# The last layer norm of a two-block transformer kernel: means by one-column products, no copies out of PSUM, and two blocks by ScalarE and GpSimd

## The reference

```python
def _layer_norm(x, g, b):
    xf = x.astype(jnp.float32)
    mu = jnp.mean(xf, axis=-1, keepdims=True)
    var = jnp.mean(jnp.square(xf - mu), axis=-1, keepdims=True)
    return ((xf - mu) * lax.rsqrt(var + LN_EPS) * g + b).astype(x.dtype)
...
        h = x * (1.0 + scale2) + shift2
        y = _conv_ffn(h, w_up[l], conv_w[l], conv_b[l], w_down[l])
        x = _layer_norm(DEEPNORM_ALPHA * x + gate2 * y, ln2_g[l], ln2_b[l])
```

## Time and profile before

| | before |
|---|---|
| median of 3 runs | 1812.11 us (1811.92 to 1812.45) |
| the profiled execution: its time | 1814.47 us |
| the profiled execution: its span | 1812.70 us |
| PE busy, share of the span | 1765.8 us, 97% |
| DVE busy | 972.2 us, 54% |
| ACT busy | 674.5 us, 37% |
| POOL busy | 825.2 us, 46% |
| granted TensorE clock, mean | 0.989 of 2.4 GHz |

### The profile page before, as it was taken

How to read it: one execution, slowest core, us unless ns; L and a number is a source line. 1 busy time by engine, 2 the same in 40 slices (tenths; PEclk the granted TensorE clock), 3 DMA queues, 4 the chain that set the end, 5 groups by cost and what they waited for, 6 DMA issues and landing times. The chain is left out here.

```text
span 1812.7 us, 26173 instructions
## 1 busy us (share of the span) xinstructions
PE 1765.8 (97%) x8981; PEld 1496.2 (83%) x8981; DVE 972.2 (54%) x1608; ACT 674.5 (37%) x1390; POOL 825.2 (46%) x664
## 2 busy tenths in 40 slices
PE   7999999999999999999999999899999899999996
PEld 5888888888777888888888888699988878888886
DVE  4257535668965477152125367466567673552545
ACT  4322222243476433232233233655532552332332
POOL 3553454567970455444545455100034465455450
PEclk9999999999999999999999999999999999999998
DMA  6454452533311345433333333100012134323321
GB/s 203 126 164 151 140 152 81 174 99 111 94 43 40 121 148 188 136 91 107 100 89 107 103 95 93 47 2 1 1 58 83 47 99 134 101 85 105 95 79 47
DMA packets 279700, 178.49 MB, mean 98 GB/s; under 512 B 6264, under 2 KB 258356, under 8 KB 279476
## 3 DMA queue, kind: packets, MB, share of 16 engines
q1 hardware_dynamic: 265348, 149.35, 28.3%
q10 hardware_dynamic: 14256, 27.87, 4.4%
HBM read 175.11 MB, written 2.10 MB: 98 GB/s over the span
## 5 line engine op out<-in xcount | busy, mean ns | idle before, releaser
L630 POOL TENSOR_TENSOR wL<-raw,wH 128x512 fp32r<-128x512 f32 (+2 forms) x560 | 747.6, 1358 | 916.7 <-ACT wH L1358 915.4
L731 PE MATMUL ps<-actH,wH 128*128 128x512 f32 (+1 forms) x1312 | 511.8, 390 | 8.1 <-DVE actL L2254 4.4
L731 PE MATMUL ps<-actH,wL 128*128 128x512 f32 (+1 forms) x1312 | 506.0, 386 | 0.0
L731 PE MATMUL ps<-actL,wH 128*128 128x512 f32 (+1 forms) x1312 | 506.0, 386 | 0.0
L1358 ACT ACTIVATE wH<-raw 128x512 fp32r<-128x512 f32 (+2 forms) x560 | 312.7, 608 | 339.6 <-PE ps L731 337.7
L731 PEld LDWEIGHTS ps<-actH,wH 128*128 128x128 f32 x1312 | 248.3, 189 | 58.8 <-issue 4.5
L731 PEld LDWEIGHTS ps<-actH,wL 128*128 128x128 f32 x1312 | 248.3, 189 | 49.6
L731 PEld LDWEIGHTS ps<-actL,wH 128*128 128x128 f32 x1312 | 248.2, 189 | 49.3 <-issue 0.7
L731 PE MATMUL ps<-hidH,wH 128*128 128x512 f32 (+1 forms) x720 | 267.6, 372 | 0.0
L731 PE MATMUL ps<-hidH,wL 128*128 128x512 f32 (+1 forms) x720 | 266.6, 370 | 0.0
L731 PE MATMUL ps<-hidL,wH 128*128 128x512 f32 (+1 forms) x720 | 266.5, 370 | 0.0
(11 more groups left out here) (320 smaller groups left out, 2037.6 us busy)
## 6 DMA issues: line engine op xcount, KB each, us to landing
mod_raw<-in_w_mod ACTq DMA_DIRECT2D x24, 1024.0 KB, 5.8
raw<-in_w_in SPq DMA_DIRECT2D x48, 512.0 KB, 3.7
raw<-in_ffn_w_gate SPq DMA_DIRECT2D x44, 512.0 KB, 3.9
raw<-in_ffn_w_up SPq DMA_DIRECT2D x44, 512.0 KB, 3.8
raw<-in_w_up SPq DMA_DIRECT2D x44, 512.0 KB, 3.8
raw<-in_ffn_w_down SPq DMA_DIRECT2D x32, 512.0 KB, 3.8
raw<-in_w_out SPq DMA_DIRECT2D x16, 512.0 KB, 3.7
raw<-in_w_down SPq DMA_DIRECT2D x16, 512.0 KB, 3.6
```

Source lines behind the costliest of these rows:

```text
L630: nc.gpsimd.tensor_tensor(wL[:, b:b + w // 2], raw[:, b:b + w // 2], wH[:, b:b + w // 2].bitcast(F32), ALU.subtract).then_inc(lo_ready, 1)
L731: return nc.tensor.matmul(out, a, b, start=first, stop=last)
```

## The change

It does these things:

- The means of the tokens come from TensorE. `mean_columns(pair, b, ks)` multiplies a 128x128 piece of x by one column of `ones` (which holds 1/1024), for two token blocks and the feature tiles `ks`, and puts each result in a column of its own in bank b. VectorE adds the eight columns of a token block with one `tensor_reduce`.
- The blocks of half 1 of the features are no longer copied to SBUF. ACT squares them, and `gained_block` reads them, in PSUM.
- TensorE's transposes move: those of blocks 4 and 5 into the middle of slab 0 of half 1, behind 16 one-column products; two of the four pieces of blocks 6 and 7 to before the last slab, behind 12 products. After the last slab there are four transposes and four products.
- For q = 2 and 3 and half 0 of the features, `gained_block` leaves VectorE: ACT subtracts the mean (`Identity` with a bias, after its squares) and GpSimd multiplies with the gain. `last_block` waits for it.
- `c_bias` is made before the drain of the last slab of half 0; the blocks of q = 1 are finished before the second pair begins.

```diff
+        pool.wait_ge(gb_in, 32)
+        for q in range(2, ST):
+            pool.wait_ge(fin_shift, q - 1)
+            G.tensor_tensor(out_block(q), out_block(q), ln2_gB[:, 0:512], ALU.mult).then_inc(fin_gained, 1)
...
-        def natural(n, tiles, ready):
+        def natural(n, ks=range(4)):
 
             half, q = n // ST, n % ST
-            for k in range(4):
-                pe.wait_ge(*ready(k))
+            for k in ks:
                 mm = nc.tensor.transpose(bank(4 + q, P, k * P), x[:, (4 * half + k) * S + q * P:][:, 0:P], ident)
-            mm.then_inc(fin_T, 1)
+            if 3 in ks:
+                mm.then_inc(fin_T, 1)
+
+        def mean_columns(pair, b, ks):
+
+            for q in (2 * pair, 2 * pair + 1):
+                for k in ks:
+                    mm = product(ps[:, b, (q % 2) * KT + k:][:, 0:1], x[:, k * S + q * P:][:, 0:P], ones[:, 0:1], True, True)
+            if KT - 1 in ks:
+                mm.then_inc(fin_cols, 1)
...
-            def hook(half, j):
-                if half == 0 and j in (1, 2):
+            def hook(half, j, k):
+                if half == 0 and j in (1, 2) and k == K - 1:
+                    pe.wait_ge(drained_v, d0 + 4)
                     for q in (2 * j - 2, 2 * j - 1):
-                        natural(q, range(4), lambda k: (drained_v, d0 + k + 1))
-                if half == 1 and j == 1:
+                        natural(q)
+                if (half, j, k) == (1, 0, 3):
+                    pe.wait_ge(fin_sum, ST)
+                    pe.wait_ge(half_drained, 2 * 4)
+                    mean_columns(0, 6, range(KT))
                     for q in range(2):
-                        pe.wait_ge(fin_sum, q + 1)
-                        natural(ST + q, range(4), lambda k: (half_drained, 4 + k + 1))
+                        natural(ST + q)
+                if (half, j, k) == (1, 2, K - 1):
+                    pe.wait_ge(fin_centre, 1)
+                    pe.wait_ge(drained_v, d0 + 6)
+                    mean_columns(1, 0, range(6))
+                    for q in range(2, ST):
+                        natural(ST + q, (0, 1))
 
             token_halves("f3_down2", ready, K, 4, lambda j, k: None, hook)
-            for q in range(2, ST):
-                pe.wait_ge(fin_sum, q + 1)
-                natural(ST + q, range(4), lambda k: (drained_v, d0 + 4 + k + 1))
+            for k in (2, 3):
+                pe.wait_ge(drained_v, d0 + 4 + k + 1)
+                for q in range(2, ST):
+                    natural(ST + q, (k,))
+                mean_columns(1, 0, (4 + k,))
...
             if n >= ST:
-                act.wait_ge(fin_copy, q + 1)
+                act.wait_ge(fin_T, n + 1)
...
-            nc.scalar.activation(tile(sq2, n % 2), out_block(n), ACT.Square, scale=D ** -0.5, bias=ssq[:, 8 + q:9 + q],
+            nc.scalar.activation(tile(sq2, n % 2), bank(4 + q) if n >= ST else out_block(n), ACT.Square, scale=D ** -0.5, bias=ssq[:, 8 + q:9 + q],
                                  accum_out=ssq[:, 32 + n:33 + n]).then_inc(fin_sq, 1)
+        act.wait_ge(fin_centre, 3)
+        for q in range(2, ST):
+            nc.scalar.activation(out_block(q), out_block(q), ACT.Identity, bias=ssq[:, 20 + q:21 + q]).then_inc(fin_shift, 1)
...
-        def final_mean(q0):
-
-            for q in (q0, q0 + 1):
-                dve.wait_ge(fin_T, ST + q + 1)
-                V.tensor_tensor_reduce(out=out_block(ST + q), in0=bank(4 + q),
-                                       in1=zero[:, 0:1].broadcast_to([P, S]), scale=1.0, scalar=0.0,
-                                       op0=ALU.add, op1=ALU.add, accum_out=rest[:, q:q + 1]).then_inc(fin_copy, 1)
-            dve.wait_ge(fin_copy, q0 + 2)
-            two = slice(q0, q0 + 2)
-            link(V.scalar_tensor_tensor(md[:, two], rest[:, two], 1.0 / D, c_half[:, two], ALU.mult, ALU.add))
-            link(V.tensor_tensor(mu_neg[:, two], c_neg[:, two], md[:, two], ALU.subtract))
+        def final_mean(pair, b):
+
+            two = slice(2 * pair, 2 * pair + 2)
+            dve.wait_ge(fin_cols, pair + 1)
+            V.tensor_reduce(mean[:, two], bank(b, 2 * KT).rearrange("p (q k) -> p q k", q=2), AX_X, ALU.add).then_inc(fin_centre, 1)
+            dve.wait_ge(fin_centre, pair + 1)
+            link(V.tensor_tensor(md[:, two], mean[:, two], c_neg[:, two], ALU.add))
...
+            if half == 0 and q >= 2:
+                dve.wait_ge(fin_gained, q - 1)
             V.scalar_tensor_tensor(o, o, rn[:, q:q + 1], ln2_bB[:, half * 512:half * 512 + 512],
                                    ALU.mult, ALU.add).then_inc(fin_v, 1)
...
-        for j in range(2):
-            half_tile("f3_down2", 1, j, 40, 4)
+        half_tile("f3_down2", 0, 3, 40, 4)
+        half_tile("f3_down2", 1, 0, 40, 4)
         dve.wait_ge(gb_in, 32)
-        final_mean(0)
-        for half in range(2):
-            gained_block(0, half)
+        final_mean(0, 6)
+        gained_block(0, 0)
+        gained_block(1, 0)
+        gained_block(0, 1)
+        half_tile("f3_down2", 1, 1, 40, 4)
+        gained_block(1, 1)
         final_rn(0)
         half_tile("f3_down2", 1, 2, 40, 4)
-        for half in range(2):
-            last_block(0, half)
+        last_block(0, 0)
+        last_block(0, 1)
         half_tile("f3_down2", 1, 3, 40, 4)
-        final_mean(2)
-        for half, q in ((0, 1), (1, 1), (0, 2), (0, 3), (1, 2), (1, 3)):
-            gained_block(q, half)
-        final_rn(2)
-        for q in range(1, ST):
+        last_block(1, 0)
+        last_block(1, 1)
+        final_mean(1, 0)
+        V.tensor_scalar(ssq[:, 22:24], mean[:, 2:4], -1.0, None, ALU.mult).then_inc(fin_centre, 1)
+        gained_block(2, 1)
+        gained_block(3, 1)
+        final_rn(1)
+        for q in range(2, ST):
             for half in range(2):
                 last_block(q, half)
```

More of the change, by code:

```diff
@@ L395, in _build @@
     conv_c, conv_act = sem("conv_c"), sem("conv_act")
-    fin_T, fin_sum, fin_mean, fin_sq, fin_copy = (sem(n) for n in (
-        "fin_T", "fin_sum", "fin_mean", "fin_sq", "fin_copy"))
+    fin_T, fin_sum, fin_mean, fin_sq, fin_cols, fin_centre = (sem(n) for n in (
+        "fin_T", "fin_sum", "fin_mean", "fin_sq", "fin_cols", "fin_centre"))
+    fin_shift, fin_gained = sem("fin_shift"), sem("fin_gained")
     half_done, half_drained = sem("half_done"), sem("half_drained")
@@ L1327, in _ @@
         token_halves("out2", (hid_ready, 2 * (NF + KT) - KT), KT, 0, provisional_mean,
-                     lambda half, j: moments(0) if (half, j) == (1, 0) else spread_moments(0) if (half, j) == (1, 2) else None)
+                     lambda half, j, k: None if k < KT - 1 or half == 0 else
+                     moments(0) if j == 0 else spread_moments(0) if j == 2 else None)
         up_down("f3", 2 * (NF + KT), None)
@@ L2347, in _ @@
             gated_tile("f3_down2", 0, j, 40)
-        total, c_bias, c_half, c_neg = ssq[:, 0:ST], ssq[:, 8:8 + ST], ssq[:, 12:12 + ST], ssq[:, 16:16 + ST]
-        rest, md, m2, mu_neg = ssq[:, 20:20 + ST], ssq[:, 24:24 + ST], ssq[:, 28:28 + ST], ssq[:, 40:40 + ST]
-        squares, var = (ssq[:, 32:32 + ST], ssq[:, 36:36 + ST]), small[:, 0:ST]
-        def final_mean(q0):
-            for q in (q0, q0 + 1):
-                dve.wait_ge(fin_T, ST + q + 1)
-                V.tensor_tensor_reduce(out=out_block(ST + q), in0=bank(4 + q),
-                                       in1=zero[:, 0:1].broadcast_to([P, S]), scale=1.0, scalar=0.0,
-                                       op0=ALU.add, op1=ALU.add, accum_out=rest[:, q:q + 1]).then_inc(fin_copy, 1)
-            dve.wait_ge(fin_copy, q0 + 2)
-            two = slice(q0, q0 + 2)
-            link(V.scalar_tensor_tensor(md[:, two], rest[:, two], 1.0 / D, c_half[:, two], ALU.mult, ALU.add))
-            link(V.tensor_tensor(mu_neg[:, two], c_neg[:, two], md[:, two], ALU.subtract))
@@ L2365, in gained_block @@
-        def gained_block(q, half):
-            o = out_block(half * ST + q)
-            dve.wait_ge(fin_sq, half * ST + q + 1)
-            V.scalar_tensor_tensor(o, o, mu_neg[:, q:q + 1], ln2_gB[:, half * 512:half * 512 + 512], ALU.add, ALU.mult)
-        def final_rn(q0):
-            two = slice(q0, q0 + 2)
+        total, c_bias, c_neg, mean = ssq[:, 0:ST], ssq[:, 8:8 + ST], ssq[:, 12:12 + ST], ssq[:, 16:16 + ST]
+        md, m2, squares, var = ssq[:, 24:24 + ST], ssq[:, 28:28 + ST], (ssq[:, 32:32 + ST], ssq[:, 36:36 + ST]), small[:, 0:ST]
@@ new lines, in final_mean @@
+        def final_mean(pair, b):
[4 more added lines that the diff above has]
+            link(V.tensor_tensor(md[:, two], mean[:, two], c_neg[:, two], ALU.add))
+        def gained_block(q, half):
+            n = half * ST + q
+            dve.wait_ge(fin_sq, n + 1)
+            V.scalar_tensor_tensor(out_block(n), bank(4 + q) if half else out_block(n), mean[:, q:q + 1],
+                                   ln2_gB[:, half * 512:half * 512 + 512], ALU.subtract, ALU.mult)
@@ L2374, in final_rn @@
```

(8 more changed lines are left out.)

6 lines of the change are left out of this document (3 added, 3 removed).

## The result

The changed kernel takes 1818.66 us (median of 7 runs, 1818.36 to 1819.07); the kernel before, run beside it, 1812.45 us (7 runs, 1811.50 to 1814.52). The ratio is 1.003, with a 95% interval of 1.0021 to 1.0040: slower by 0.21 to 0.40%. The forecast was 1811.6 us, in a range of 1809.4 to 1813.6. It was wrong, on the other side of no change.

What follows compares the result with a forecast made beforehand. TensorE sets the pace until about 1795, then VectorE's list to the end. VectorE's tail net of TensorE's delay −2.4 us, GpSimd blocking VectorE +1.9, together −0.5 off the 1812.11 median: 1811.6 us, range 1809.4 to 1813.6.

Steps and rivals of the forecast that it cites:

- One-column products exist in the trace: eight of them took from 399.87 to 400.68, 0.101 us each.: TensorE's added products: unit price read from an earlier row, about 0.1 us for each one-column product.
- The last slab ends 3.3 us later.: TensorE, last half: short instructions grow from 0.87 to 4.2 us, so the last drain of x starts 1.85 us later.
- the 1.45 us of slack that I had found: Last drain of x: VectorE starts it at 1796.70, last matmul issued at 1794.91; TensorE's added time first eats this wait.
- The rival with the clock: TensorE's clock falls after the short instructions: one fall costs 1.5 us, 1813.1, chance 0.12; low for most of the rest, 0.03.
- the stretch of 1240 to 1260: Earlier TensorE trace, held against a clock fall: clock stays 1.00 though 1.9 us short runs alternate with 0.8 us wide ones.
- it decides the sign of the result: TensorE's clock fall: claimed from 59 slow matmuls of the 84 left, at 0.07 us each; all 84 would give 1817.5.
- All of this is covered by TensorE, with 1.85 us to spare.: VectorE's first-pair work before the last drain: done by 1796.7, then waits for TensorE until 1798.55, so it costs nothing.
- VectorE's tail: VectorE from the last drain of x at 1798.55 to the end at 1810.3 if nothing interferes: 2.4 us less.
- The hold: VectorE's last small operations reading SBUF twice are blocked by GpSimd's two products: adds 1.8 to 1.9 us; chance 0.60.
- The first ends with the first product, the second with the second: VectorE's `md × md` and variance end with GpSimd's products, at 1803.1 and 1804.4, the latter instead of 1802.6.
- ACT late, waits for GpSimd: Rival: a 1.28 us table load before `Identity`, within 0.3 us of forecast, chance 0.05; VectorE's waits for GpSimd forecast as hidden.
- I take the difference off the median: Final step: the 0.5 us shorter span is subtracted from the runs' median of 1812.11, giving 1811.6.

Runs made afterwards that it cites:

- the chain in PSUM: Changed kernel with half of the one-column products and one operand of the last pair's small VectorE operations in PSUM: 1810.62 us, ratio 0.9989 to the kernel before.
- changed, chain in PSUM: Changed kernel, all its products kept, with one operand of the last pair's small VectorE operations in PSUM: 1817.69 us, ratio 1.0026 to the kernel before.

## Why the prediction was wrong

- **"One-column products exist in the trace: eight of them took from 399.87 to 400.68, 0.101 us each."** This step failed. The earlier trace rows shows eight instructions, and `row_sums` issues four products (one for each of the four token blocks). A product is two instructions, so it costs 0.20 us by that row and not 0.10; in the changed kernel's two runs it costs 0.22. Two experiments bear this out: with 16 products fewer the last drain starts 5.13 us earlier, and with 16 added to the kernel before 5.09 us later, each time 3.5 us of products and 1.6 of the clock. I took the count of a row for the count of calls, though the function behind the row says otherwise. The Trainium skill, "FP8 and Floating Point Precision", section "TensorE Precision Notes", says that true fp32 takes four passes through the array; the profile here shows two matmuls for a product, each with its load, and no run resolves what is inside them. The wide products of this kernel are split by hand and count once.
- **"The last slab ends 3.3 us later."** With the right price: 28 products at 0.218 are 6.1 us instead of 2.8. Everything else in the term stands: 0.5 for the four transposes and the ends of the runs. That makes 6.6, less the 1.45 us of slack that I had found, 5.15 us for the last drain. With 1.6 for the clock it is 6.75, and measured it is 6.69.
- **The rival with the clock.** I gave one fall a chance of 0.12 and 1.5 us; it is there in all six profiles with 16 products in slab 0, and in the changed kernel costs 1.6 us (0.57 on the transposes, 1.0 on ten matmuls). The chance was wrong. The size came out near, partly by luck: I took 0.07 us more for each slow matmul from a window whose count of 16 takes in matmuls that reach over its edges. Inside it they start every 0.213 us (1426.27 to 1428.83 for twelve), 0.09 more, and here it is 0.10; the 0.4 that I added for the edges made up for it. What I held against a fall, the stretch of 1240 to 1260, has runs of 1.9 us between wide ones; the products here took 3.5 us and not the 1.6 that I had priced. With half of the products they take 1.7 us, and the clock stays. So the wrong price also made the comparison with that stretch look closer than it was. That the right price would have led me to a high chance is not shown. I also wrote that from 59 slow matmuls on "it decides the sign of the result". That is where 59 × 0.07 = 4.1 us reach 0.2% above the kernel before; the sign itself changes once they cost 0.5 us, at seven. A second fall, which comes in some executions, I had not seen as a rival of its own.
- **"All of this is covered by TensorE, with 1.85 us to spare."** The order of VectorE held as forecast; it had more to spare, 3.21 us, since TensorE was later still.
- **VectorE's tail.** This part was right, and the change did there what it was meant to do. The reduce took 0.17 us (estimate 0.2). I forecast 13.65 us from the last drain to the end of the span, with the hold; measured were 13.29.
- **The hold.** "The first ends with the first product, the second with the second": measured 0.95 and 1.18 us for `md × md` and the variance, 1.8 us together above their normal time, as priced. The row that I gave for an operation spared by its input in PSUM was weak, since that operation started 0.09 us ahead of GpSimd's; the chain in PSUM starts inside GpSimd's work and shows it. Taken away alone (changed, chain in PSUM) it gives back 1.56 net of the operation that this costs.
- **ACT late, waits for GpSimd.** Neither came: no table load stands ahead of `Identity`, and `last_block` never waits for `fin_gained`.

- **"I take the difference off the median".** That left the time outside the span as it was. The offload adds 0.34 us to it, a term that the sum put at nothing.

With the right price of 0.22 us a product, the same sum gives −0.5 + 3.3 = 2.8 us more than before without a fall (1814.9 us) and 4.4 with one, both outside the range that I gave. With one fall, the 0.36 us that the last part came out shorter, and the 0.34 outside the span it is 4.4 us, of the 6.2 measured. The second fall, 1.5 us where it comes, is most of what is left; no run shows how often it comes.

## What to carry to other kernels

Before a row's time is divided by its count, count the calls in the code that made it: an fp32 matmul can be two instructions, and a one-column product then costs two loads of 128x128 weights, 0.22 us, however little it computes. Work that is moved to an engine which sets the pace has to be priced there by the instruction; here halving it, by using sums that another engine had already made, turned +4.0 us of tail into −0.9. The offload to GpSimd shortened the tail by 1.05 us where what VectorE did meanwhile read SBUF at most once, and lengthened it by 0.5 to 0.7 us where it didn't. Ask too what lies outside the profile's span: here the offload added 0.34 us there, and the difference of an execution's time and its span, which is at hand for every execution, shows it.

## What the runs showed of the hardware that was not expected

- A product of an fp32 tile of 128x128 with one column is recorded as two loads and two matmuls; each pair takes 0.10 us in a run of eight records and 0.11 in the runs of 24 and 32, at the full clock.
- TensorE's granted clock falls from 2.4 to 1.2 GHz within a stretch in which the profile calls TensorE busy without a gap: with 16 such products in slab 0, in six of six profiles; with eight, in none of four. In the one profile with the 16 spread among wide matmuls the loss was larger: 1.00 less the clock, times the 2 us of each of the four windows from 1786, is 3.4 us of full clock, and 1.7 us where they stand in one run. What in such work the clock answers to was not isolated: the width of the products was not varied.
- Two operations of VectorE on 128x2 elements took 0.95 and 1.18 us beside GpSimd's products of 128x512, and 0.15 to 0.17 without them; with one operand in PSUM they ran in 0.16 and 0.17 beside the same products.
- With `Identity` on ACT and two products on GpSimd near the end, an execution is 2.13 us longer than its span, and 1.79 us without: the ranges of 73 and 112 executions don't touch.
